# Stick-breaking rounds of a one-core kernel: the absolute value moved to VectorE, ScalarE's functions regrouped

## The reference, cut to what matters

```python
def _stick_breaking(q, k, v):                      # (B, H, S, d), 8 heads of 64
    for blk in range(seq // QBLOCK):               # 4 query blocks of 128
        z = jnp.einsum('bhtd,bhsd->bhts', q[:, :, t0:t1], k[:, :, :t1]) * scale
        mask = jnp.arange(t1)[None, :] < jnp.arange(t0, t1)[:, None]
        log1m = jnp.where(mask, -jax.nn.softplus(z), 0.0)
        suffix = lax.cumsum(log1m, axis=3, reverse=True)
        a = jnp.where(mask, jnp.exp(z + suffix), 0.0)
        outs.append(jnp.einsum('bhts,bhsd->bhtd', a, v[:, :, :t1]))

def _even_mixer(h, w_in, w_out, ln_g, ln_b, sg_w, sg_b, qn_g, kn_g):
    p = h @ w_in
    za = jax.nn.gelu(p[..., :2 * A_WIDTH])         # u and vg, 512 columns each
    ...                                            # vg: layer norm, spatial mixing by sg_w
    y_a = (u * mixed).reshape(bsz, seq, A_WIDTH)   # the gated half
    q = _rmsnorm(...); k = _rmsnorm(...)           # per head
    y_b = _stick_breaking(q, k, v)
    return jnp.concatenate([y_a, y_b], axis=-1) @ w_out
```

## Time and profile before

| | |
|---|---|
| median of 3 runs | 1933.31 us (1931.28 to 1933.7) |
| profiled execution | 1930.21 us |
| its span, first to last instruction | 1928.3 us |
| mean granted TensorE clock | 0.989 |
| busy: PE, DVE, ACT, POOL | 1852.9, 953.4, 754.6, 72.9 us |

### The profile page before, as it was taken

One profiled execution on the slowest core, in us unless ns is written; L12 is line 12 of the kernel. 1 busy time (PEld: TensorE's weight loads), 2 busy tenths in 40 slices (PEclk: granted clock), 3 DMA queues, 4 the chain that ended last, 5 costly groups with the idle time before them and its releaser, 6 DMA issues.

```text
span 1928.3 us, 21089 instructions
## 1 busy us (share of the span) xinstructions
PE 1852.9 (96%) x8624; PEld 1502.4 (78%) x8624; DVE 953.4 (49%) x1363; ACT 754.6 (39%) x1066; POOL 72.9 (4%) x94
## 2 busy tenths in 40 slices
PE   3999999899999999888999999999999999999999
PEld 2788788678888888766688888888876788888887
DVE  7377636553434365545454444445644654344443
ACT  4366542342323243366643223233445443233231
POOL 5100000000000000000000000000001000000000
PEclk9999999999999999998999999999999999999999
DMA  7455553222322223200132232222221123222322
GB/s 256 163 175 183 168 168 131 87 79 97 103 94 99 99 92 113 75 33 23 44 110 99 87 102 95 98 99 98 89 85 47 55 95 102 98 99 89 105 91 77
DMA packets 55120, 197.65 MB, mean 102 GB/s; under 512 B 6400, under 2 KB 6656, under 8 KB 55024
## 3 DMA queue, kind: packets, MB, share of 16 engines
q1 hardware_dynamic: 52272, 188.24, 28.9%
q0 software_dynamic: 2320, 7.31, 1.4%
q10 hardware_dynamic: 432, 0.74, 0.1%
HBM read 194.13 MB, written 2.14 MB: 102 GB/s over the span
## 4 chain that ended last, share of the span: by engine, by line
PE 89%; DVE 5%; ACT 4%; issue 1%; DMA 1%; POOL 0%; SPq 0%; ACTq 0%; DVEq 0%
PE ps L283 26%; PE ps L284 25%; PE ps L285 25%; PE ps L319 2%; PE ps L320 2%; PE ps L321 2%; DVE RAW L1293 1%; PE ps L386 1%; PE ps L602 1%; PE ps L735 1%; PE ps L642 1%; ACT WH L832 1%; DVE WL L1285 1%; DVE ARENA L1593 1%; PE ps L337 1%
## 5 line engine op out<-in xcount | busy, mean ns | idle before, releaser
L283 PE MATMUL ps<-R0h,WH 128*128 128x512 f32 x1200 | 471.9, 393 | 21.1 <-POOL R0l L1868 18.7
L1285 DVE TENSOR_TENSOR WL<-RAW,WH 128x1024 fp32r<-128x1024 f32 x303 | 372.2, 1232 | 215.4 <-ACT WH L832 211.5
L832 ACT ACTIVATE WH<-RAW 128x1024 fp32r<-128x1024 f32 x303 | 317.7, 1052 | 408.6 <-PE ps L285 354.7
L285 PE MATMUL ps<-R0h,WL 128*128 128x512 f32 x1200 | 468.1, 390 | 0.0
L284 PE MATMUL ps<-R0l,WH 128*128 128x512 f32 x1200 | 468.1, 390 | 0.0
L283 PE MATMUL ps<-R1h,WH 128*128 128x512 f32 x1064 | 418.6, 393 | 6.0 <-POOL R1l L1898 3.1
L285 PE MATMUL ps<-R1h,WL 128*128 128x512 f32 x1064 | 415.0, 390 | 0.0
L284 PE MATMUL ps<-R1l,WH 128*128 128x512 f32 x1064 | 414.8, 390 | 0.0
L283 PEld LDWEIGHTS ps<-R0h,WH 128*128 128x128 f32 x1200 | 226.0, 188 | 74.8 <-issue 15.2
L285 PEld LDWEIGHTS ps<-R0h,WL 128*128 128x128 f32 x1200 | 225.9, 188 | 47.6
L284 PEld LDWEIGHTS ps<-R0l,WH 128*128 128x128 f32 x1200 | 226.2, 188 | 45.9
(11 more groups left out here) (270 smaller groups left out, 1391.4 us busy)
## 6 DMA issues: line engine op xcount, KB each, us to landing
RAW<-in_W SPq DMA_DIRECT2D x351, 512.0 KB, 3.2
XT<-in_X SPq DMA_DIRECT2D x4, 512.0 KB, 7.9
ARENA<-bias_scratch POOLq DMA_DIRECT2D x8, 256.0 KB, 4.4
XT<-in_X POOLq DMA_DIRECT2D x8, 256.0 KB, 3.7
out_x<-XT SPq DMA_DIRECT2D x8, 256.0 KB, 2.0
ARENA<-bias_scratch POOLq DMA_DIRECT2D x8, 128.0 KB, 3.7
con<-in_CON POOLq DMA_DIRECT2D x1, 578.0 KB, 5.8
CSB<-in_CV ACTq DMA_DIRECT2D x1, 512.0 KB, 6.0
```

Source lines behind the costliest of these rows:

```text
L283: e.matmul(ps(b), wh, hi, start=first, stop=False)
L285: return e.matmul(ps(b), wl, hi, start=False, stop=last)
L832: e.activation(WH[:, n % NHL, :], RAW[:, i % NRAW, :], ACT.Copy).then_inc(sem["w_hi"])
L1285: e.tensor_tensor(WL[:, s, :], RAW[:, i % NRAW, :], r32(WH[:, s, :]), ALU.subtract).then_inc(sem["w_lo"])
```

## The change

- Abs on ACT is replaced by min(-z, z) on DVE (`st_nab`), and ACT's Exp takes it without a scale. In even rounds it stands between the reads of the two heads' scores; in odd rounds between the two `st_zd`.
- ACT's softplus is split into `st_soft_exp` and `st_soft_ln`. In odd rounds the Exp of the head two before and the softplus Exp come first, then `hi()`, the square root of the norms, then Ln. The Exp of an even head moves to the start of the next even round.
- The reciprocal of the norms (`head_recip`) stands apart from their scaling and follows `lo()`, ahead of `st_sp`. In round 5 `head_apply` comes ahead of `eu`.
- The gated half of a chunk is in three parts in two rounds: scaling and Gelu in one, then product, high copy and remainder in the next.
- The five `scale_x` go from ahead of L1651 to round 0, behind `lo()`.
- PE's, POOL's and SP's lists are as they were.

ACT's list (diff, cut):

```diff
-            def st_soft(h):
-                L, Z = SPR[h % 2], ZR[h % 4]
-                e.wait_ge(sem["z"], 3 * h + 3)
-                if h > 1:
-                    e.wait_ge(sem["suf"], 3 * (h - 2) + 3)
-                e.activation(L, Z, ACT.Abs).then_inc(sem["abs"])
-                e.wait_ge(sem["abs"], h + 1)
-                e.activation(L, L, ACT.Exp, scale=-1.0).then_inc(sem["sxp"])
+            def st_soft_exp(h):
+                e.wait_ge(sem["nab"], h + 1)
+                e.activation(SPR[h % 2], SPR[h % 2], ACT.Exp).then_inc(sem["sxp"])
+
+            def st_soft_ln(h):
                 e.wait_ge(sem["sxp"], h + 1)
-                e.activation(L, L, ACT.Ln, bias=1.0).then_inc(sem["sln"])
+                e.activation(SPR[h % 2], SPR[h % 2], ACT.Ln, bias=1.0).then_inc(sem["sln"])
...
+            def eu_hi(n):
+                j = 2 + n % 2
                 e.wait_ge(sem["um"], n + 1)
                 e.activation(A[0][:, n, :], TMP[:, j, :], ACT.Copy).then_inc(sem["u_hi"])
...
                     if n == 8:
+                        st_exp(6)
                         hi()
+                        eu_hi(2)
                         st_exp(7)
                     elif n % 2 == 0:
+                        if n:
+                            st_exp(n - 2)
                         hi()
-                        st_soft(n)
+                        if n > 5:
+                            eu_hi(n - 6)
+                        st_soft_exp(n)
+                        st_soft_ln(n)
                     elif n < 9:
                         if n > 1:
                             st_exp(n - 2)
+                        st_soft_exp(n)
+                        hi()
                         if n < 6:
                             head_sqrt((n + 1) // 2)
-                        hi()
-                        st_exp(n - 1)
-                        st_soft(n)
+                        elif n > 5:
+                            eu_hi(n - 6)
+                        st_soft_ln(n)
+                    if n == 9:
+                        eu_hi(3)
```

DVE's list (diff, cut):

```diff
+            def st_nab(h):
+
+                Z = ZR[h % 4]
+                e.wait_ge(sem["z"], 3 * h + 3)
+                if h > 1:
+                    e.wait_ge(sem["suf"], 3 * (h - 2) + 3)
+                else:
+                    e.wait_ge(sem["mx"], 4)
+                e.scalar_tensor_tensor(SPR[h % 2], Z, -1.0, Z, ALU.mult, ALU.min).then_inc(sem["nab"])
...
                 lo(3)
-                for k in range(3, KT):
-                    scale_x(k)
...
                 for n in range(10):
+                    if n > 5:
+                        eu_mix(n - 6)
                     if n == 8:
                         st_zd(7)
+                        lo()
+                        eu_rest(2)
                     elif n % 2 == 0:
                         st_z(n)
+                        st_nab(n)
                         st_z(n + 1)
+                        lo()
+                        if n == 0:
+                            for k in range(3, KT):
+                                scale_x(k)
+                        if n > 5:
+                            eu_rest(n - 6)
+                        st_sp(n)
                     elif n < 9:
                         if n > 1:
                             st_zd(n - 2)
+                        st_nab(n)
                         st_zd(n - 1)
                         if n < 6:
                             head_norm((n + 1) // 2)
-                    if n < 9:
                         lo()
-                    if n < 8:
+                        if n < 6:
+                            head_recip((n + 1) // 2)
+                        if n > 5:
+                            eu_rest(n - 6)
                         st_sp(n)
...
-                    elif n in (1, 3, 5):
-                        c = (n + 1) // 2
-                        if c < 3:
-                            even_rr(2 * c + 2, 0)
-                        else:
-                            eu(0)
-                        head_apply(c)
-                    elif n in (2, 4):
-                        even_rr(n + 3, 1)
-                    elif n < 9:
+                    elif n < 5:
+                        even_rr(n + 3, (n + 3) % 2)
+                    if n in (1, 3, 5):
+                        head_apply((n + 1) // 2)
+                    if 5 <= n < 9:
                         eu(n - 5)
+                    if n == 9:
+                        eu_rest(3)
```

More of the change, by code:

```diff
@@ L1565, in head_norm, with head_recip @@
                                     ALU.add).then_inc(sem["hn"])
+            def head_recip(c):
                 h = HN[:, 16 * c:16 * c + 16]
@@ L1605, in eu, with eu_mix, eu_rest @@
                 e.tensor_tensor(TMP[:, j, :], ps(n % 2), SQ[:], ALU.mult).then_inc(sem["u_rr"])
+            def eu_mix(n):
+                j = 2 + n % 2
                 e.wait_ge(sem["u_g"], n + 1)
                 e.tensor_tensor(TMP[:, j, :], TMP[:, j, :], MX[:, n, :], ALU.mult).then_inc(sem["um"])
-                rest(A, n, TMP[:, j, :], ("u_hi", n + 1), "u_lo")
+            def eu_rest(n):
+                rest(A, n, TMP[:, 2 + n % 2, :], ("u_hi", n + 1), "u_lo")
             def even():
@@ L1620, in even @@
                 head_norm(0)
+                head_recip(0)
                 e.wait_ge(sem["spr"], 4)
```

## The result

The changed kernel takes 1900.43 us (1899.21 to 1900.85); before, on the same chip, 1933.51 us. The ratio is 0.983 with a 95% interval of 0.9813 to 0.9847. The profiled execution took 1899.21 us, its span is 1897.3.

A forecast was written before the change was run, and what follows sets the result against it. PE, busy 96%, bounds the kernel; its even-mixer waits cost their length and slow matmuls. Waits 22.3 plus clock 10.5 gain 32.8 us: profiled 1930.2 becomes 1897.4, plus 3.1 for the median, 1900.5; range 1895 to 1912.

The forecast's parts named there:

- The steps for the stage: Even mixer, 798.5 to 948.3: shorter PE waits (22.3 us) plus full-clock matmuls (10.5 us) gain 32.8 us.
- The waits: PE's waits in the even mixer, for head_apply, L1651 and st_sp: 25.3 us before, 22.3 of it to go.
- the two named: First pair's remaining PE waits: 2.2 us ahead of st_b(0), 0.75 for head_apply in its odd round.
- The clock: Even mixer: granted clock back to 1.00, saving 8.2 on scores, 1.5 on st_b(7)'s L642, 0.8 on multiplications: 10.5 us.
- The four score bursts: PE's scores of the four head pairs (L602): 17.8 us before, 2.4 each at full clock, saving 8.2 (6.0 to 8.6).
- MoBA's burst, the bound for the full clock: MoBA's scores, also 2560 columns on 64 rows, took 2.95 us at clock 1.00: upper bound for a score burst.
- The rounds: From the scores' end, st_sp ends at 8.5 us (even), 20.2 (odd), 20.5 (round 7), covered by PE's work.
- The new pass: st_nab on DVE, replacing ACT's Abs: 1.5 us each, as st_sp; two table loads fewer in the stage.
- waits of about 3 us and more: Even mixer: the low clock shows only behind such PE waits, so waits of at most 2.2 us leave 1.00.
- a clock that stays low without waits: Rival: score bursts stay slow although the waits are short; gain about 24 us, 1909; chance 0.17.
- waits that come back elsewhere: Rival: handovers or nab take 1 us more per round, PE waits in most rounds; 1912 to 1925; chance 0.06.
- the slow min: Rival, slower: eight nab passes in the chain; at 6.3 us each the gain is gone; chance 0.04.

The follow-up runs named there:

- fill: Kernel before, with 18, 11 and 20 extra unused matmuls on PE during the waits ahead of the second, third and fourth pair's scores: 1927.76 us, ratio 0.9976.
- group_only: Kernel before with only ACT's new order, Abs still on ACT, scale_x and gated half as before: 1911.36 us.
- u_group: Changed kernel with ACT's old order back; the min on DVE and the rest stay: 1910.48 us.
- u_scale: Changed kernel with the five scale_x back ahead of the first mix: 1905.1 us.
- delay5: Changed kernel with five extra dependent DVE passes, results unused, ahead of head_apply in rounds 1, 3 and 5: 1909.79 us.
- nab_only: Kernel before with only the absolute value moved from ACT to DVE (st_nab): 1923.16 us.
- round01: Changed kernel with round 0's weight split and remainder behind softplus, scale_x ahead of st_sp(0), round 1's spread mid-multiplication, head_apply ahead of even_rr: 1895.7 us against 1900.57.
- delay7: Changed kernel with seven extra dependent DVE passes, results unused, ahead of head_apply in rounds 1, 3 and 5: 1917.37 us.

## Why the prediction was right

1900.5 us was forecast, 1900.43 measured. The steps for the stage hold one by one: it became 32.6 us shorter, 32.8 were forecast. That the medians agree to a tenth of a microsecond is luck, as the last two points say.

- *The waits.* 21.9 us went (22.3 forecast). The two that stayed are the two named: 2.47 (2.2) and 0.89 us (0.75).
- *The clock.* The four score bursts lost 7.8 us (8.2), L642 of st_b(7) 1.4 (1.5); PE's busy time in the stage fell by 10.8 (10.5) to 113.7. That the waits bring the low clock was an inference from rows; fill and the delays show it from both sides. MoBA's burst, the bound for the full clock, lies behind the stretch that the prediction points to (175 to 190); the clock is 1.00 at 197.3 to 200.3 too. By the Trainium skill (TensorE: Matmul & The Clock Gate, A second HAM failure mode) frequent small idles between groups of matmuls can make the clock swing between its levels. The changed kernel has two short waits left in the stage, and its clock there is 1.00, so the trace shows no swing; behind the longer waits of the experiments the clock fell, though not each time.
- *The rounds.* st_sp(2) ends 8.6 us behind the scores (8.5); st_sp(3) 20.15 behind the same scores, at 852.07 (20.2); st_sp(7) 20.5 behind the scores that end at 884.66 (20.5). PE starts st_b(7) at 905.18, 0.05 behind that end: just covered, as the prediction says.
- *The new pass.* 1.50 us (1.5), and 24 table loads (8 + 7 + 4 + 3 + 2) instead of 26. Ln starts 0.02 us behind its load in round 2, and the load 0.02 behind the Exp. The Trainium skill (ScalarE: Activation LUTs, What ACT_TABLE_LOAD costs) has a drain of about 1380 ns with each load; this trace doesn't show it. By an estimate from that figure st_sp(2) would have been later by 1.4 us.
- *The parts.* Not the pass that moved to DVE carries most of the gain, but ACT's order: alone it gives 20.9 us, undone it costs 10.1. The parts don't add up: alone three give 35.8 together, undone the four cost about 20, because min and order both relieve the odd rounds, and what one of them frees is spare time for the other. The wait ahead of the second pair shows it: 5.18 us before, 3.90 with the min alone, 1.27 with the order alone, 0.89 with both. The gated half in parts was only undone, never put in alone, and the reciprocal's new place was tested by no run.
- *What was off: the clock.* The low clock was expected only behind waits of about 3 us and more, so that 2.2 would be safe. Behind 2.17 us (group_only), 2.47 (u_group, u_scale, delay5) and 2.62 (nab_only, where L642 of st_b(7) took 3.91) it came. In the changed kernel's profiled execution its wait of 2.47 us was followed by the full clock. That was luck, worth 1.2 to 1.7 us by the slow cases, and the measured time would have been in the range without it.
- *What was off: outside the stage.* The profiled execution was forecast at 1897.4 and took 1899.21, 1.8 more. The stage began 1.0 us later than before, and what follows it took 0.6 longer. Over all profiled executions, before and after, the stage begins between 798.5 and 799.5, so the first is within the spread between executions; the cause of the 0.6 is open. To get from the profiled execution to the median the prediction added 3.1, as before; it was 1.2 here, 1.9 less. The two misses cancel.

Of the rivals, a clock that stays low without waits and waits that come back elsewhere are refuted by the bursts of 2.46 us and the list of waits; the slow min by its 1503 ns.

## What to carry to other kernels

Lay each engine's queue against the work of the engine that is the bound, round by round, with durations of the trace: an edit is worth what it takes from the chain beyond that cover, here little for eight passes once the order was right, and nearly two thirds of the gain for the order alone. Where TensorE waits, price the wait and the slow matmuls behind it; a fill with useless matmuls tells the two apart. And look at what a queue's head waits for, as ACT's weight split in round 0, before moving work between engines: round01 moved it, and the wait behind it was gone.

## What was not expected of the hardware

The clock behind a wait is not the same from one execution to the next. Behind the same wait of 2.47 us ahead of st_b(0), L642 took 2.42 us in the changed kernel, delay7 and nab_only, and 3.64, 3.83 and 4.11 in u_group, u_scale and delay5; up to there delay5 and delay7 run the same instructions as the changed kernel. Behind 3.33 us the first scores took 2.61 in u_scale and 4.11 in group_only. In this stage's profiles all score bursts behind waits up to 1.9 us took 2.46; behind 2.17 to 3.64 us bursts and L642 came out at either level; behind 3.76 to 5.8 us every score burst was slow (3.94 to 4.64). So a wait of 2 to 4 us has to be priced with and without the low clock.

The DVE pass with two SBUF inputs took 1.60 us instead of 1.49 in the one round in which it began while POOL's last addition still ran. The other profiled kernels with this order show 1.60 to 1.61 too; in round01, where POOL had ended 0.1 us before, the pass took 1.48. That POOL is the cause fits this, but no run was made to test it. DVE's and POOL's rows of the changed kernel:

```profile
816.73 1.60 DVE L1611 SCALAR_TENSOR_TENSOR ARENA<-ARENA 128x1280 f32<-128x1280 f32 x1
```

```profile
816.53 0.45 POOL L1952 TENSOR_TENSOR ARENA<-ARENA 128x128 f32<-128x128 f32 x1
```
